# Second attentions of a two-layer kernel: one head of each pair scaled on VectorE, two bias tables and the latent norms in other places

## The chip, the cores and the metric

The kernel runs on one core of a Trainium2 chip. The metric is the device time of one execution in microseconds (us). All of the work is in float32.

## The reference, cut to what matters

The program computes two transformer blocks, one after the other, over 512 tokens of width 1024. The change lies in the mixing stage of the second block:

```python
z = rms_norm_2(h, mix_pre_g) @ w_in
q_na, k_na, v_na, c_q, c_kv, k_rope = jnp.split(z, split_at, axis=-1)
o_na = neighbourhood_attention(q_na, k_na, v_na, na_rpb)     # 8 heads
o_mla = latent_attention(c_q, c_kv, k_rope, ...)             # 8 heads
mixed = concat([rms_norm_2(o_na, g1), rms_norm_2(o_mla, g2)]) @ w_out

def latent_attention(...):
    q = rms_norm_2(c_q, q_norm_g) @ w_uq       # 256 -> 8 x 96
    kv = rms_norm_2(c_kv, kv_norm_g) @ w_ukv   # 128 -> 8 x 128
    q_rot, k_rot = apply_rope(q_rot), apply_rope(k_rope)
    p = softmax((qn @ k_nope.T + qr @ k_rot.T) * scale)
    return p @ v
```

In the neighbourhood attention a query sees 256 keys and each head adds a bias table made from `na_rpb`. In the latent attention a query sees all 512 keys.

## The kernel before, in words

Everything is written out by hand, one program for each engine, and the engines meet through counting semaphores. The tokens are four tiles of 128. Before the attentions the projections (`z2_psum`, `z2_evac`) run on TensorE in four groups n, each with two weight units of raw float32 that ScalarE (L402) and VectorE (L408) split into a high and a low part; three products (L417 to L419) make one float32 product. Units are numbered from `AT_MID`: 0 to 7 are `w_in`, 8 and 9 the latent up-projections, 10 to 13 `w_out`. SyncE loads a unit (`feed`, L714) once the unit two before it is split.

Both attentions ("na", the neighbourhood attention, then "mla", the latent attention) go through the same four functions, `attend_pe`, `attend_dve`, `attend_act` and `attend_pool`. A phase has 32 steps, one for a head and a tile of 128 queries. Round d (16 of them, and two more to drain, `LAG` is 2) takes steps 2d and 2d + 1, the same tile of the two heads of a pair. I call them head a and head b. In a round each engine does, in this order:

- TensorE: the transposes of the probabilities of round d - 2 (L542, waits for `scaled`), the score products of round d (L553, waits until both scores of round d - 1 are taken), and, once in four rounds, the head outputs from the transposed probabilities (L571).
- VectorE: score plus bias with the running maximum (L603) for step 2d; then the reciprocal (L583) of the sum of step 2d - 1; then L603 for 2d + 1; then the reciprocal of 2d. In rounds 5, 9, 13 and 17 it also takes the low part of a pair's output (L1848, L1851), and waits for TensorE and ScalarE before.
- ScalarE: copies of the transposes of round d - 2 (L635), then the exponentials of steps 2d and 2d + 1 with their sums (L645), and the high part of the output (L1484, L1486) in rounds 5, 9, 13 and 17.
- GpSimd: each step's probabilities times the reciprocal, in place (L660).

In the neighbourhood attention a bias table of a head is one product (L1306) and three additions on VectorE (L2115). Tables 0 and 1 come ahead of the rounds and table 2 at the opening of round 0, so three are made before the first score is taken. The others come two in four rounds. TensorE waits ahead of them for `band_in`: 32 transfers, issued by GpSimd (L957), that lay the values v2 out in bands (`Vband`). They must land before the attention because the probabilities buffer `PB2` lies where v2 was. VectorE in the meantime does the norms of the two latents: eight squares with sums (L2096), a square root on ScalarE, eight scalings (L2104).

Between the attentions come the transposes of the latents, the up-projections, the rotations of k and q on VectorE (L2133 to L2138; q's four tiles after the last copy of k, L2145) and the transposes per head (L1352). Then VectorE splits units 10 and 11 of `w_out` ahead of the first latent score.

## Time and profile before

| | us |
|---|---|
| median of three runs (lowest) | 2055.45 (2053.97) |
| profiled execution | 2055.96, of which span 2054.1 |
| first to last projection of the stage | about 1305 to 1391 |
| end of projections to the first neighbourhood score | 1391 to 1410 |
| neighbourhood attention, first score to last head outputs | 1410.1 to 1465.5 |
| norm sums, latent transposes and projections, rotations | 1469 to 1512 |
| latent attention, first score to last head outputs | 1518.0 to 1592.6 |

Times within the span count from its start. The stage with the change is about an eighth of the span. TensorE is busy 88% of the whole span but much less between 1391 and 1600.

### The profile page before, as it was taken

How to read it: one execution, taken by the hardware profiler on the slowest of the kernel's cores; microseconds unless marked ns; L12 is line 12 of the kernel's file. 1: busy time of each engine (PE TensorE's matmuls, PEld its weight loads, DVE VectorE, ACT ScalarE, POOL GpSimd, SP SyncE). 2: the span in 40 equal slices, each digit the busy share in tenths (PEclk: the TensorE clock that was granted, in tenths of full speed). 3: DMA queues.
4: the chain of work that ended last, by engine and by line, in shares of the span. 5: the costliest groups of instructions: out<-in, count | busy, mean ns of one | idle time of the engine just before them, and what ended most of it. 6: DMA issues, size and time to landing. Idle time of an engine off the chain costs nothing.

```text
span 2054.1 us, 22543 instructions
## 1 busy us (share of the span) xinstructions
PE 1816.5 (88%) x8515; PEld 1439.0 (70%) x8515; DVE 925.0 (45%) x1469; ACT 853.1 (42%) x1348; POOL 294.6 (14%) x374
## 2 busy tenths in 40 slices
PE   5996999999769999939999999696767959999996
PEld 4884666668658888828888887583643748888885
DVE  3446334334359999942322323525243352322324
ACT  3224565552348888832223222324456132223221
POOL 2100442220001111200000000623236000000000
PEclk9998899999779999969999999897789979999998
DMA  5223101115369999642324332331010113324321
GB/s 178 97 75 107 48 22 57 47 42 217 131 220 375 387 382 379 225 164 82 102 73 112 92 102 73 103 110 52 1 41 1 52 52 103 102 81 114 85 100 52
DMA packets 160930, 248.37 MB, mean 121 GB/s; under 512 B 11490, under 2 KB 117057, under 8 KB 147904
## 3 DMA queue, kind: packets, MB, share of 16 engines
q1 hardware_dynamic: 151056, 230.21, 33.2%
q0 software_dynamic: 9776, 16.86, 2.7%
q8 instruction: 62, 1.02, 0.2%
q14 instruction: 36, 0.29, 0.0%
HBM read 241.22 MB, written 12.61 MB: 124 GB/s over the span
## 4 chain that ended last, share of the span: by engine, by line
PE 84%; DVE 8%; issue 2%; ACT 2%; POOL 2%; DMA 2%; SPq 0%; DVEq 0%; ACTq 0%
PE psum L417 24%; PE psum L419 23%; PE psum L418 23%; PE psum L553 3%; PE psum L571 3%; PE psum L542 2%; POOL arena L660 2%; DVE tarea_r L1711 1%; DMA warea<-in_w_in 1%; DVE harea L1683 1%; ACT warea_r L402 1%; PE psum L1161 1%; DVE harea L1698 1%; DVE xarea L1700 1%; PE psum L1071 1%
## 5 line engine op out<-in xcount | busy, mean ns | idle before, releaser
L408 DVE TENSOR_TENSOR warea_r<-warea,warea_r 128x2048 fp32r<-128x2048 f32 x114 | 266.5, 2339 | 409.0 <-ACT warea_r L402 408.9
L417 PE MATMUL psum<-tarea_r,warea_r 128*128 128x512 f32 x896 | 358.3, 400 | 13.4 <-DVE tarea_r L1711 13.4
L418 PE MATMUL psum<-tarea_r,warea_r 128*128 128x512 f32 x896 | 352.6, 394 | 0.0
L419 PE MATMUL psum<-tarea_r,warea_r 128*128 128x512 f32 x896 | 352.2, 393 | 0.0
L402 ACT ACTIVATE warea_r<-warea 128x2048 fp32r<-128x2048 f32 x114 | 217.5, 1910 | 287.0 <-PE psum L419 282.6
L417 PE MATMUL psum<-warea_r,arena_r 128*128 128x512 f32 (+1 forms) x768 | 300.7, 392 | 12.1 <-DVE arena_r L2010 7.3
L419 PE MATMUL psum<-warea_r,arena_r 128*128 128x512 f32 (+1 forms) x768 | 297.1, 387 | 0.0
L418 PE MATMUL psum<-warea_r,arena_r 128*128 128x512 f32 (+1 forms) x768 | 297.0, 387 | 0.0
L417 PEld LDWEIGHTS psum<-tarea_r,warea_r 128*128 128x128 f32 x896 | 170.5, 190 | 54.5 <-DVE tarea_r L1711 14.1
L419 PEld LDWEIGHTS psum<-tarea_r,warea_r 128*128 128x128 f32 x896 | 170.5, 190 | 36.4
L418 PEld LDWEIGHTS psum<-tarea_r,warea_r 128*128 128x128 f32 x896 | 170.7, 190 | 33.9
L1573 ACT ACTIVATE arena<-psum 128x512 f32<-128x512 f32 x44 | 26.3, 599 | 370.2 <-PE psum L419 370.2
L417 PEld LDWEIGHTS psum<-warea_r,arena_r 128*128 128x128 f32 (+1 forms) x768 | 143.6, 187 | 44.0 <-DVE arena_r L2010 7.9
L419 PEld LDWEIGHTS psum<-warea_r,arena_r 128*128 128x128 f32 (+1 forms) x768 | 143.3, 187 | 29.3
L418 PEld LDWEIGHTS psum<-warea_r,arena_r 128*128 128x128 f32 (+1 forms) x768 | 143.6, 187 | 28.1
L2057 DVE TENSOR_TENSOR arena<-psum,arena 128x512 f32<-128x512 f32 x44 | 30.4, 692 | 290.4 <-ACT arena L1573 290.4
L417 PE MATMUL psum<-warea_r,tarea_r 128*128 128x512 f32 (+3 forms) x408 | 156.7, 384 | 1.4 <-DVE tarea_r L2126 1.4
L418 PE MATMUL psum<-warea_r,tarea_r 128*128 128x512 f32 (+3 forms) x408 | 155.8, 382 | 0.0
L419 PE MATMUL psum<-warea_r,tarea_r 128*128 128x512 f32 (+3 forms) x408 | 155.7, 382 | 0.0
L973 PE MATMUL psum<-const,harea 128*128 128x128 f32 x160 | 29.2, 368 | 86.6 <-DVE harea L1683 86.6
L660 POOL TENSOR_SCALAR arena<-arena,rr 128x256 f32<-128x256 f32 (+1 forms) x64 | 78.8, 1242 | 122.5 <-DVE rr L583 122.3
L635 ACT ACTIVATE harea<-psum 128x128 f32<-128x128 f32 (+4 forms) x192 | 73.6, 419 | 48.7 <-PE psum L542 48.0
(291 smaller groups left out, 2438.5 us busy)
## 6 DMA issues: line engine op xcount, KB each, us to landing
warea<-in_ffn_w_gu SPq DMA_DIRECT2D x88, 512.0 KB, 5.0
warea<-in_w_in SPq DMA_DIRECT2D x48, 512.0 KB, 4.6
warea<-in_ffn_w_down SPq DMA_DIRECT2D x40, 512.0 KB, 4.2
arena<-in_w_up SPq DMA_DIRECT2D x16, 1024.0 KB, 7.6
tarea<-in_w_up SPq DMA_DIRECT2D x16, 1024.0 KB, 7.1
tarea<-in_w_down SPq DMA_DIRECT2D x16, 1024.0 KB, 7.6
warea<-in_w_gate SPq DMA_DIRECT2D x14, 1024.0 KB, 7.5
harea<-in_w_gate SPq DMA_DIRECT2D x14, 1024.0 KB, 7.8
```

Of the source, the lines that this page charges most:

```text
L402: act.activation(w_hi[:, u % 2, :], raw[:, u % RAW, :], ACT.Copy).then_inc(s["split_hi"], 1)
L408: dve.tensor_tensor(w_lo[:, u % 2, :], raw[:, u % RAW, :], w_hi[:, u % 2, :].bitcast(f32), ALU.subtract)\
L417: nc.tensor.matmul(out, high, by_high, start=first, stop=False)
L418: nc.tensor.matmul(out, high, by_low, start=False, stop=False)
L419: return nc.tensor.matmul(out, low, by_high, start=False, stop=last)
L542: mm = nc.tensor.transpose(bank[0:rows, P * j:P * j + P], pbuf[:, c0:c0 + rows], ident)
L553: mm = nc.tensor.matmul(ps[st["e"]][:, a:b], st["lhsT"], rhs, start=True, stop=not (mask and b == n))
L571: mm = nc.tensor.matmul(half(bank, e_)[:, c:d_], lhsT, PT[0:lhsT.shape[0], e_, j, a:b], start=start, stop=stop)
L635: nc.scalar.activation(PT[0:rows, st["e"], 0:nj, st["dst"]:st["dst"] + P], src, ACT.Copy)\
L660: ins = nc.gpsimd.tensor_scalar(p, p, rr[:, k:k + 1], None, ALU.mult)
L973: mm = nc.tensor.transpose(ps[2 * t + half_][:, P * c:P * c + P], hn[:, t, P * (4 * half_ + c):P * (4 * half_ + c) + P], ident)
L2057: V.tensor_tensor(sgb[:, v % 2, :], ps[2 * (v % 2) + 1], sgb[:, v % 2, :], ALU.mult).then_inc(s["gated"], 1)
```

## The change

1. In the two second attentions head b's probabilities are scaled on VectorE, at the opening of the next round, ahead of that round's scores. GpSimd scales head a only. A new semaphore `scaled_dve` counts VectorE's, and `scaled(n)` tells who waits for which. The first attention keeps its order.
2. The neighbourhood tables 0 and 1 are multiplied in the last group of projections (into banks 0 and 1), and VectorE makes them before it splits units 8 and 9.
3. The latent norms go from ahead of the attention into its rounds: squares in rounds 2 to 5, the root in ScalarE's round 6, scalings in rounds 8 to 11.
4. The 32 band transfers go to SyncE's queue, behind unit 9; TensorE waits for them only ahead of the first head outputs. `PB2` and the scratch `zsq` move to the gain area, and `load_gain(5)` goes behind the attention.
5. q is rotated tile by tile during the up-projections; TensorE waits only for the last copy of k.
6. Units 10 and 11 are split inside the latent attention: ScalarE in rounds 2 and 5, VectorE in rounds 3 and 6.

```diff
-    v2, PB2 = carve(8192, NT, 512), carve(8192, 4, T)
+    v2, PB2 = carve(8192, NT, 512), whole(G_AT + 1024, 4, 256)
+    def scaled(n):
+        if n < alone:
+            return s["scaled"], n + 1
+        return (s["scaled_dve"], (n - alone) // 2 + 1) if (n - alone) % 2 else (s["scaled"], alone + (n - alone) // 2 + 1)
...
@@ attend_pe
-                    pe.wait_ge(s["scaled"], n0 + m + 1)
+                    pe.wait_ge(*scaled(n0 + m))
...
+                if ph["name"] == "na" and u == 0:
+                    pe.wait_ge(s["band_in"], 16 * 32)
...
@@ attend_dve
+            if n0 >= alone and 0 <= 2 * d - 1 < len(steps):
+                m = 2 * d - 1
+                recip(m)
+                p = ph["pb"][:, (n0 + m) % 4, 0:steps[m]["keys"]]
+                dve.wait_ge(s["recd"], n0 + m + 1)
+                nc.vector.tensor_scalar(p, p, rr[:, k:k + 1], None, ALU.mult).then_inc(s["scaled_dve"], 1)
             for m in range(2 * d, 2 * d + 2):
...
-                if 0 <= m - 1 < len(steps):
+                if 0 <= m - 1 < len(steps) and (n0 < alone or m % 2):
                     recip(m - 1)
...
@@ attend_pool
+            if n0 >= alone and m % 2:
+                continue
...
@@ sync
             for u in range(AT_MID, AT_FFN2):
                 feed(u)
+                if u == AT_MID + 9:
+                    sp.wait_ge(s["z2_evac"], 12)
+                    for b, band in enumerate((0, 8, 24, 32)):
+                        for r in range(8):
+                            sp.dma_start(Vband[...], v2[...]).then_inc(s["band_in"], 16)
...
@@ tensor
+                    if n == 3 and h == 0:
+                        pe.wait_ge(s["xrev_in"], 16 * 8 * H)
+                        for g in range(2):
+                            pe.wait_ge(s["z2_evac"], 8 + g + 1)
+                            na_table(g, ps[g])
-            pe.wait_ge(s["band_in"], 16 * 32)
+            pe.wait_ge(s["na_tab"], 2)
             attend_pe(pe, na, na_table)
...
-            pe.wait_ge(s["cn_ready"], 1)
+            pe.wait_ge(s["cn_ready"], 4)
...
-            pe.wait_ge(s["roped"], 2)
+            pe.wait_ge(s["roped"], 1)
...
@@ scalar
-            root(rstd[:, 16:24])
-            attend_act(act, na, pair_high(...))
+            def latent_root(d):
+                if d == 6:
+                    root(rstd[:, 16:24])
+            attend_act(act, na, pair_high(...), split=latent_root)
...
-            split_high(AT_MID + 10)
-            split_high(AT_MID + 11)
-            attend_act(act, mla, pair_high(...))
+            def out_high(d):
+                if d in (2, 5):
+                    split_high(AT_MID + 10 + d // 5)
+            attend_act(act, mla, pair_high(...), split=out_high)
...
@@ vector
-            for k in range(2, 10):
+            for k in range(2, 8):
                 split_low(AT_MID + k)
+            for g in range(2):
+                na_table(g, ps[g])
+            split_low(AT_MID + 8)
+            split_low(AT_MID + 9)
+            attend_dve(dve, na, pair_low(...), na_table, latent_norm)
...
             for t in range(NT):
+                dve.wait_ge(s["mla_evac"], 4 * t + 2)
+                rope(q_[:, :, 64:80], q_[:, :, 80:96], ct, st_, [P, H, 16], 128)
                 dve.wait_ge(s["mla_evac"], 4 * t + 4)
                 ins = V.tensor_copy(kf[...], view(z3[:, t, 384:416], [[0, H], [1, 32]]))
...
-            split_low(AT_MID + 10)
-            split_low(AT_MID + 11)
-            attend_dve(dve, mla, pair_low(...))
+            def out_low(d):
+                if d in (3, 6):
+                    split_low(AT_MID + 10 + d // 6)
+            attend_dve(dve, mla, pair_low(...), fill=out_low)
```

`latent_norm(d)` does for tile d - 2 the two squares (d 2 to 5), the variances (d 5), the inverse root (d 7) and for tile d - 8 the two scalings (d 8 to 11).

How this moves the instructions, on VectorE at the first scores of the neighbourhood attention. Before (L2104 is the last of the latent norms, L2115 a table, L603 a score, printed as ISA, with its maximum; L583 a reciprocal):

```order
L2104 SCALAR_TENSOR_TENSOR arena<-arena,rstd,small 128x128
L2106 MEMSET nmax 128x1
L2115 TENSOR_TENSOR arena<-psum,const 128x256 x9
L603 ISA arena,nmax<-psum,arena 128x256
L603 ISA nmax 128x1
L603 ISA arena,nmax<-psum,arena 128x256
L603 ISA nmax 128x1
L583 RECIPROCAL rr<-sums 128x1
L2115 TENSOR_TENSOR garea<-psum,const 128x256 x3
L603 ISA arena,nmax<-psum,arena 128x256
L603 ISA nmax 128x1
L583 RECIPROCAL rr<-sums 128x1
```

and of the changed kernel, from the split of the last projection units on (L408 the split, L2152 a table, L621 the score, L594 the reciprocal, L609 the new scaling, L2129 a latent's square):

```order
L408 TENSOR_TENSOR warea_r<-warea,warea_r 128x2048 x6
L2152 TENSOR_TENSOR arena<-psum,const 128x256 x6
L408 TENSOR_TENSOR warea_r<-warea,warea_r 128x2048 x2
L2152 TENSOR_TENSOR arena<-psum,const 128x256 x3
L621 ISA garea,nmax<-psum,arena 128x256
L621 ISA nmax 128x1
L621 ISA garea,nmax<-psum,arena 128x256
L621 ISA nmax 128x1
L594 RECIPROCAL rr<-sums 128x1
L2152 TENSOR_TENSOR garea<-psum,const 128x256 x3
L594 RECIPROCAL rr<-sums 128x1
L609 TENSOR_SCALAR garea<-garea,rr 128x256
```

Six table additions now stand ahead of the last two splits, three remain ahead of the first score, and head b's scaling stands ahead of the next score. Its round 2 from the scaling of round 1's head b to head b's reciprocal, with the first squares:

```order
L609 TENSOR_SCALAR garea<-garea,rr 128x256
L621 ISA garea,nmax<-psum,arena 128x256
L621 ISA nmax 128x1
L621 ISA garea,nmax<-psum,arena 128x256
L621 ISA nmax 128x1
L594 RECIPROCAL rr<-sums 128x1
L2129 ISA garea,ss<-arena 128x256
L2129 ISA ss 128x1
L2129 ISA garea,ss<-arena 128x128
L2129 ISA ss 128x1
L594 RECIPROCAL rr<-sums 128x1
```

The squares stand between the reciprocals of head a and head b.

VectorE in the latent attention, rounds 0 and 1. Before (L2156 copies of the transposes per head):

```order
L2156 COPY arena<-psum 96x512 x8
L408 TENSOR_TENSOR warea_r<-warea,warea_r 128x2048 x2
L603 ISA arena,nmax<-psum,arena 128x512
L603 ISA nmax 128x1
L603 ISA arena,nmax<-psum,arena 128x512
L603 ISA nmax 128x1
L583 RECIPROCAL rr<-sums 128x1
L603 ISA arena,nmax<-psum,arena 128x512
L603 ISA nmax 128x1
L583 RECIPROCAL rr<-sums 128x1
L603 ISA arena,nmax<-psum,arena 128x512
```

and now, from the scaling of round 2's head b to that of round 3, with the split of unit 10:

```order
L594 RECIPROCAL rr<-sums 128x1 x2
L609 TENSOR_SCALAR arena<-arena,rr 128x512
L621 ISA arena,nmax<-psum,arena 128x512
L621 ISA nmax 128x1
L621 ISA arena,nmax<-psum,arena 128x512
L621 ISA nmax 128x1
L594 RECIPROCAL rr<-sums 128x1
L408 TENSOR_TENSOR warea_r<-warea,warea_r 128x2048
L594 RECIPROCAL rr<-sums 128x1
L609 TENSOR_SCALAR arena<-arena,rr 128x512
```

The two splits no longer stand ahead of the first score; one stands between the reciprocals of head a and head b of round 3, the other likewise in round 6.

## Rows read from the trace of the kernel before

**Rows 1.** Three stretches by engine: us, busy time (x) of PE, PEld, DVE, ACT, POOL, PEclk, DMA share, GB/s
```profile
1390.00:1404.00 14.00, 2.47 (x7) 1.00 (x5) 9.85 (x32) 3.81 (x4) 0.00 (x0) 0.65 0.49 141
1425.00:1438.40 13.40, 10.19 (x71) 6.04 (x69) 7.38 (x34) 8.27 (x26) 7.29 (x8) 0.87 0.00 1
1538.70:1557.40 18.70, 14.75 (x67) 7.33 (x68) 7.22 (x26) 11.97 (x27) 12.41 (x8) 1.00 0.00 0
```

**Rows 2.** Timeline, VectorE and TensorE, from the projections to the first score (start us, us, what)
```profile
1393.24 2.29 DVE L408 TENSOR_TENSOR warea_r<-warea,warea_r 128x2048 fp32r<-128x2048 f32 x1 [7.06 <-ACT warea_r L402]
...
1399.53 3.60 DVE L2104 SCALAR_TENSOR_TENSOR arena<-arena,rstd,small 128x256 f32<-128x256 f32 x8
...
1404.30 1.65 PE L1306 MATMUL psum<-arena,const 128*128 128x384 f32 x2 [7.84 <-DVE arena L2115]
...
1405.99 1.09 DVE L2115 TENSOR_TENSOR arena<-psum,const 128x256 f32<-128x256 f32 x3 [1.74 <-PE psum L1306]
...
1410.06 0.42 DVE L603 CUSTOM_DVE_ANT_0 arena<-psum,arena 128x256 f32<-128x256 f32 x1 [0.16 <-DVE arena L2115]
```

**Rows 3.** Timeline of first rounds, neighbourhood attention: ScalarE, GpSimd, VectorE, TensorE
```profile
1411.04 0.49 ACT L645 ACTIVATE arena<-arena,nmax 128x256 f32<-128x256 f32 x1
...
1411.43 0.92 POOL L660 TENSOR_SCALAR arena<-arena,rr 128x256 f32<-128x256 f32 x1 [22.02 <-DVE rr L583]
...
1415.70 0.42 DVE L603 CUSTOM_DVE_ANT_0 arena<-psum,arena 128x256 f32<-128x256 f32 x1 [1.94 <-PE psum L553]
...
1416.30 1.82 POOL L660 TENSOR_SCALAR arena<-arena,rr 128x256 f32<-128x256 f32 x2 [1.38 <-DVE rr L583]
...
1417.37 0.66 PE L542 MATMUL psum<-const,arena 128*128 128x128 f32 x2 [1.08 <-POOL arena L660]
...
1417.96 1.22 PE L553 MATMUL psum<-arena 64*128 64x256 f32 x4
...
1419.21 0.42 DVE L603 CUSTOM_DVE_ANT_0 arena<-psum,arena 128x256 f32<-128x256 f32 x1 [2.25 <-PE psum L553]
```

**Rows 4.** Timeline, TensorE: last head outputs of the neighbourhood attention
```profile
1465.54 3.68 PE L571 MATMUL psum<-harea,arena 128*64 128x128 f32 x32 [0.47 <-ACT harea L635]
```

**Rows 5.** Timeline, VectorE and TensorE, between the latent projections and the latent attention
```profile
1495.40 0.29 DVE L2145 COPY harea<-arena 128x256 f32<-128x256 f32 x1 [3.18 <-ACT arena L1631]
...
1501.60 6.20 PE L1352 MATMUL psum<-const,arena 128*96 128x128 f32 x32 [6.92 <-DVE nmax L2152]
...
1512.36 1.96 PE L553 MATMUL psum<-arena 96*128 96x512 f32 x4 [0.83 <-ACT arena L1636]
...
1513.62 4.50 DVE L408 TENSOR_TENSOR warea_r<-warea,warea_r 128x2048 fp32r<-128x2048 f32 x2 [1.37 <-ACT warea_r L402]
...
1518.04 0.68 DVE L603 CUSTOM_DVE_ANT_0 arena<-psum,arena 128x512 f32<-128x512 f32 x1
```

**Rows 6.** Timeline, ScalarE, GpSimd, VectorE and TensorE in the latent attention
```profile
1519.40 3.78 PE L553 MATMUL psum<-arena 96*128 96x512 f32 x4 [5.08 <-DVE nmax L603]
...
1519.49 0.70 ACT L645 ACTIVATE arena<-arena,nmax 128x512 f32<-128x512 f32 x1
...
1519.87 1.57 POOL L660 TENSOR_SCALAR arena<-arena,rr 128x512 f32<-128x512 f32 x1 [55.14 <-DVE rr L583]
...
1533.83 0.69 DVE L603 CUSTOM_DVE_ANT_0 arena<-psum,arena 128x512 f32<-128x512 f32 x1 [2.36 <-PE psum L553]
...
1537.93 0.69 DVE L603 CUSTOM_DVE_ANT_0 arena<-psum,arena 128x512 f32<-128x512 f32 x1 [2.36 <-PE psum L553]
...
1592.62 5.07 PE L571 MATMUL psum<-harea,arena 128*64 128x512 f32 x16 [0.69 <-ACT harea L635]
```

**Rows 7.** Timeline, GpSimd and VectorE in the first projections
```profile
56.08 3.60 POOL L871 TENSOR_TENSOR harea<-arena 128x2048 f32<-128x2048 f32 x1 [41.58 <-ACT arena L1432]
...
57.83 4.00 DVE L408 TENSOR_TENSOR warea_r<-warea,warea_r 128x2048 fp32r<-128x2048 f32 x1 [8.94 <-ACT warea_r L402]
```

**Rows 8.** Timeline, SyncE: issues of transfers
```profile
1377.62 0.80 SPq L714 DMA_DIRECT2D warea<-in_mla_w_ukv  x2
```

More of the change, by code:

```diff
@@ L316, in build_blocks @@
     rpbs = carve(13312, 64)
-    zsq = whole(H_AT, 256)
+    zsq = whole(G_AT + 768, 256)
     z3 = carve(16144, NT, 416)
@@ L526, in attend_pe @@
         rounds = len(steps) // 2
-        if table:
+        if table and ph["name"] != "na":
             table(0)
@@ L580, in recip @@
             if n0 + n >= 8:
-                dve.wait_ge(s["scaled"], n0 + n - 7)
+                dve.wait_ge(*scaled(n0 + n - 8))
             k = (n0 + n) % 8
             nc.vector.reciprocal(rr[:, k:k + 1], sums[:, k:k + 1]).then_inc(s["recd"], 1)
-        if table:
+        if table and ph["name"] != "na":
             table(0)
@@ L616, in attend_act @@
         rounds = len(steps) // 2
-        if table:
+        if table and ph["name"] != "na":
             table(0)
@@ L1271, in _, with na_table @@
             pe.wait_ge(s["f_evac"], 16)
+            def na_table(g, bank=ps[7]):
+                if g >= H:
+                    return
+                if g >= 2:
+                    pe.wait_ge(s["na_tab"], g)
+                nc.tensor.matmul(bank[:, 0:384], flip, xrev[:, g, :], start=True, stop=True).then_inc(s["tab_psum"], 1)
             to_features(3)
@@ L1612, in _ @@
                 split_high(AT_MID + 2 * n + 3)
-            root(rstd[:, 16:24])
-            attend_act(act, na, pair_high(na, lambda pair: o2[0][0][:, pair, :], 984, sq_na))
+            def latent_root(d):
+                if d == 6:
+                    root(rstd[:, 16:24])
+            attend_act(act, na, pair_high(na, lambda pair: o2[0][0][:, pair, :], 984, sq_na), split=latent_root)
             root(rstd[:, 24:28])
@@ L2089, in _ @@
             low_features(3)
-            for k in range(2, 10):
+            for k in range(2, 8):
                 split_low(AT_MID + k)
-            dve.wait_ge(s["z2_evac"], 16)
-            for t in range(NT):
-                for k, (a, b_) in enumerate(((0, 256), (256, 384))):
-                    ins = V.tensor_tensor_reduce(out=zsq[:, 0:b_ - a], in0=z3[:, t, a:b_], in1=z3[:, t, a:b_], scale=1.0,
-                                                 scalar=0.0, op0=ALU.mult, op1=ALU.add, accum_out=ss[:, 16 + 4 * k + t:17 + 4 * k + t])
-                    chained(ins)
@@ L2099, in _ @@
-            chained(variance(rstd[:, 16:20], ss[:, 16:20], 256))
-            variance(rstd[:, 20:24], ss[:, 20:24], 128).then_inc(s["var_ready"], 1)
-            inverse_root(rstd[:, 16:24])
-            for t in range(NT):
-                for k, (a, b_) in enumerate(((0, 256), (256, 384))):
-                    chained(V.scalar_tensor_tensor(out=z3[:, t, a:b_], in0=z3[:, t, a:b_], scalar=rstd[:, 16 + 4 * k + t:17 + 4 * k + t],
-                                                   in1=small[:, 600 + a:600 + b_], op0=ALU.mult, op1=ALU.mult))
@@ L2109, in na_table @@
+            def na_table(g, bank=ps[7]):
                 if g >= H:
```

59 lines of the change are left out of this document (33 added, 26 removed).

## Prediction

> **What bounds the kernel now.** I read the page first, then the chain of waits between 1390 and 1650 us, the busy times by stretch, and last the timelines of single rounds. The chain runs through TensorE in the rest of the kernel, and the change does not touch that. Between 1391 and 1600 it does not: in the four rounds from 1538.7 to 1557.4 TensorE is busy 14.75 of 18.7 us, and GpSimd, VectorE and ScalarE less still [rows 1]. No engine is full, so a loop of waits sets the round.
>
> In the neighbourhood attention the loop is this: VectorE takes a score at 1415.70, does head b's reciprocal behind it, GpSimd starts at 1416.30 (head b of the round before, then head a; 1.82 for both), TensorE transposes at 1417.37, multiplies the next scores from 1417.96 for 1.22, and VectorE's next score comes at 1419.21 [rows 3]. That is 3.5 us; the four rounds from 1425 took 13.4, so 3.35 each with tables and a head output [rows 1]. The point to see is that head b's reciprocal stands behind a score of the next round, which stands behind TensorE. In the latent attention the same loop takes 4.10 (1533.83 to 1537.93) [rows 6].
>
> Ahead of the attentions VectorE alone is on the chain. Its last split ends at 1395.5, the latents' norms end at 1403.1, and three tables at 1.09 each, each with a product of 1.65 in front, put the first score at 1410.06 [rows 2]. Before the latent attention there are two more such places: after the last copy of k at 1495.40 the rotations of q keep TensorE until 1501.60, and two splits keep the first latent score from about 1513.4 until 1518.04 [rows 5].
>
> **The change, part by part.** Gains have a minus.
>
> *Opening, -11.6.* The norms (7.6) and two of three tables leave the stretch. Two products join the projections ahead of the last split. At 1.65 each [rows 2], a time taken at a lower clock, they cost 3.3, at twice the clock half of it; the projections keep TensorE full, so I take 1.8. VectorE's two tables there have idle time to lie in (7.06 ahead of the last split [rows 2]). The last split then ends at 1395.5 + 1.8 = 1397.3, table 2 at 1398.4, and the first score is 11.6 earlier than 1410.06.
>
> *The new operation.* No row shows a scaling on VectorE from SBUF to SBUF. Nearest below is the copy of 128x256 in 0.29 [rows 5], above the scores at 0.42 and 0.69 [rows 2, 6]. I take 0.35 for 256 columns and 0.49 for 512, near the copy, with a little for the scalar's operand.
>
> *Does it wait for GpSimd?* In the first projections a split that takes 2.29 elsewhere [rows 2] took 4.00: it started at 57.83 while GpSimd worked from 56.08 to 59.68, and ended at 61.83, about 2.2 after GpSimd [rows 7]. So VectorE stood still until GpSimd was done. This split reads two SBUF inputs; the scaling reads one. But the copy gets 256 columns through in 0.29 where the score takes 0.42, so it uses a wider path than the score, and I take it that the wide path is the one shared. The Trainium skill says the same (SBUF — State Buffer, Who interferes with whom): GpSimd's only ports are VectorE's second pair, two-input operations and the fast form of one-input ones need it, and the first to start holds it for the whole instruction. By that rule the trace's 4.00 agrees, and the change puts the two halves of a pair on engines that can't work at once. Without the rule's one-input half the sum would be rival 1's.
>
> *A plain neighbourhood round, 2.64.* From a score to GpSimd's start 1.37 (1410.06 to 1411.43), GpSimd 0.92 [rows 2, 3], then head b's scaling 0.35, then the next score. Head b's exponential (from 1411.04) is done at about 1.60 after the score and its reciprocal at 1.76, so without the wait for GpSimd it would be 2.15. TensorE fits below: transposes 0.66 and scores 1.22 [rows 3], both released by the round before.
>
> *All neighbourhood rounds, +4.8.* Fifteen rounds at 2.64 are 39.6. Six tables lie mostly beside GpSimd: 0.3 each, 1.8. Three rounds with a head output hold VectorE behind TensorE and ScalarE as before, and the scaling comes on top: 2.2 each, 6.6. The latents' squares and scalings read two SBUF inputs, so each pair stands around GpSimd's 0.92: I take 1.1 in each of eight rounds, 8.8 (their bare work, 7.6 from 1395.5 to 1403.1 [rows 2], less what lies in idle time, is the lower bound at about 3; a GpSimd operation's 0.92 ahead of both of a pair, 1.82, the upper, 14.6). From the last score to the last head outputs 3.5 (2.64 and a transpose and a copy). Sum 60.3, against 1410.06 to 1465.54, 55.5 [rows 2, 4]. So the rounds get longer although the loop gets shorter, since 16 operations were moved into them. The root adds table loads on ScalarE; its idle time covers them. The bands' 32 issues at 0.40 [rows 8] end near 1391, and the first head outputs come after 1410: nothing.
>
> *Rotations, -5.8, and -1.* TensorE's transposes start 0.4 after the copy at 1495.40 in place of 1501.60 [rows 5]. With 6.9 less of idle time ahead, its clock should be better for the first of them (6.20 for 32): -1, between 0 and -2.
>
> *Latent opening, -4.6.* The two splits, 4.50, go. The scores' products start at 1512.36, the first head's half is done at 1513.4 [rows 5], and the score follows.
>
> *Latent rounds, -0.6.* Plain: 1518.04 to 1519.87 is 1.83, GpSimd 1.57, scaling 0.49: 3.89 against 4.10 [rows 5, 6]. Fifteen are 58.4. Three head outputs 1.8 each, 5.4 (before, 18.7 less three times 4.10 gives 6.4 for such a round; now 5.7, as TensorE is ahead). The two splits now stand between the reciprocals of a round, and GpSimd and VectorE take turns around 2.29: 2.5 each, 5.0 (0 if all is covered, 4 if GpSimd's turn comes whole on top). Tail 5.2. Sum 74.0 against 74.6 (1518.04 to 1592.62) [rows 5, 6].
>
> Sum: -11.6 + 4.8 - 5.8 - 1 - 4.6 - 0.6 = -18.8. The profiled execution took 2055.96, so 2037; the median of the runs, 2055.45, is the same within 0.5.
>
> **Rivals.**
>
> 1. *The scaling does not wait for GpSimd, the two-input operations do.* For it: the only row shows a two-input operation. Against: the copy's speed. A plain latent round is then 1519.49 + 0.80 for head b's sum, 2.3 after the score, reciprocal, scaling: 3.0; TensorE, busy 14.75 in four rounds with a head output [rows 1], needs about 3 in a plain one and makes it 3.1. The 15 rounds save 0.8 each, less what the splits take back: 7 more. The neighbourhood saves 1.5, since its rounds hold the latents' operations. -27: 2029.
> 2. *No operation waits for GpSimd there.* Then the latents' and splits' prices shrink too, 6 more: 2023. Rows 7 speak against it.
> 3. *Slower: TensorE falls to the lower clock in the latent attention.* In the neighbourhood rounds 10.19 busy of 13.4 went with 0.87, in the latent ones 14.75 of 18.7 with 1.00 [rows 1]. At the lower clock the scores' products take 3.78 [rows 6], twice their usual time, transposes grow too, and TensorE needs about 5.4 for a round: at 1.5 over 3.89, 15 rounds cost 23 more, the head outputs 6. -18.8 + 29 = +10: 2066. It turns to a loss from two thirds of that attention at 1.2 GHz on. Against it: the new rounds hold the same products in less time, so TensorE rests less.
> 4. *The bands come late.* If SyncE took 1.5 for a transfer in place of 0.40, they would land at 1428, and the first head outputs, due near 1414, would wait 14: 2051. It decides from 1.1 each on.
>
> **How the numbers follow.** Forecast 0.60; rival 1 0.20; rival 2 0.07; rival 3 0.05; rival 4 0.08. The forecast's own range is 2030 to 2044 (latents 3 to 14.6, splits 0 to 4 more, the tables' product 0.9 to 3.3, clock). The range reaches to rival 2 below and rival 4 above: 2022 to 2051. Two per cent are 41 us, about what a measurement of this kernel can tell from no change. No case but a sum of several goes beyond: faster 0.02, slower 0.01, within 0.97.
>
> **What would show it.** First neighbourhood score at about 1398; plain rounds 2.6 there with the scaling starting when GpSimd ends (longer than 0.35, as its record would include the wait); rounds 2 to 5 and 8 to 11 longest; last head outputs at about 1459. Transposes per head start 0.4 after the last copy of k. Plain latent rounds 3.9, rounds 3 and 6 over 6. A latent round near 3.1 with GpSimd and the scaling side by side would be rival 1; a split or a square at its bare time beside GpSimd rival 2; TensorE at 1.2 GHz there rival 3; TensorE waiting for a transfer ahead of the first head outputs rival 4. I am wrong in the main term if the first score doesn't come before 1400.

## The result, and the profile after

The changed kernel takes 2022.4 us (median of 4 runs, 2020.4 to 2023.3) against 2055.1 for the kernel before on the same chip: a ratio of 0.984, 95% interval 0.982 to 0.986. One of the four runs of before took 3139.5 us, which the ratio leaves out; the median of the other three is 2054.7. The profiled execution of after, the longest of its four, has a span of 2021.5, 32.6 less than before's.

The two kernels do not enter the changed part at the same time, though nothing ahead of it differs. So the stages are counted from a common mark, VectorE's weight split at 1375.30 before and 1374.08 after, the third from last of the projections, to the first split behind both attentions (1616.78 and 1585.29). This *stretch* is 241.5 us before and 211.2 after, 30.3 less. The rest of the 32.6 lies ahead of it (1.2) and behind it (1.1).

| Stage | before | after | measured | predicted |
|---|---|---|---|---|
| mark to first score | 34.8 | 22.5 | -12.3 | -11.6 |
| neighbourhood rounds, to the last head outputs | 55.5 | 55.5 | 0.0 | +4.8 |
| to the transposes per head | 36.1 | 30.3 | -5.8 | -5.8 |
| to the first latent product | 10.8 | 8.4 | -2.4 | -1 |
| to the first latent score | 5.7 | 1.2 | -4.5 | -4.6 |
| latent rounds, to the last head outputs | 74.6 | 68.9 | -5.7 | -0.6 |
| to the first split behind | 24.2 | 24.4 | +0.2 | no term |

The timeline of after at these borders (start, duration, engine, line, operation, idle time before it and who ended it). It is to be held against [rows 2, 4, 5]:

```profile
1393.37 2.29 DVE L408 TENSOR_TENSOR warea_r<-warea,warea_r 128x2048 fp32r<-128x2048 f32 x1 [7.79 <-ACT warea_r L402]
1396.58 0.41 DVE L621 CUSTOM_DVE_ANT_0 garea<-psum,arena 128x256 f32<-128x256 f32 x1
...
1452.10 3.68 PE L582 MATMUL psum<-harea,arena 128*64 128x128 f32 x32 [0.47 <-ACT harea L653]
...
1482.06 0.29 DVE L2190 COPY harea<-arena 128x256 f32<-128x256 f32 x1 [0.20 <-ACT arena L1658]
1482.40 0.32 PE L1376 MATMUL psum<-const,arena 128*96 128x128 f32 x1 [1.14 <-DVE harea L2190]
...
1490.78 1.53 PE L562 MATMUL psum<-arena 96*128 96x512 f32 x3 [0.82 <-ACT arena L1663]
...
1492.01 0.69 DVE L621 CUSTOM_DVE_ANT_0 arena<-psum,arena 128x512 f32<-128x512 f32 x1 [1.33 <-PE psum L562]
...
1560.92 1.08 PE L582 MATMUL psum<-harea,arena 128*64 128x512 f32 x4 [0.74 <-ACT harea L653]
```

See that only 0.9 us lie between the last split's end at 1395.66 and the score, where before had norms and tables, that the transposes start 0.34 after the last copy does, and that the latent score no longer has two splits ahead of it.

A plain neighbourhood round, to be held against [rows 3]: GpSimd's scaling and VectorE's new one run side by side.

```profile
1400.95 0.16 DVE L594 RECIPROCAL rr<-sums 128x1 f32<-128x1 f32 x1 [0.32 <-ACT garea L663]
1401.21 1.03 POOL L680 TENSOR_SCALAR garea<-garea,rr 128x256 f32<-128x256 f32 x1 [2.35 <-DVE rr L594]
...
1401.64 0.35 DVE L609 TENSOR_SCALAR garea<-garea,rr 128x256 f32<-128x256 f32 x1
1401.94 0.42 DVE L621 CUSTOM_DVE_ANT_0 garea<-psum,arena 128x256 f32<-128x256 f32 x1
```

VectorE starts 0.43 us into GpSimd's operation and is through in 0.35; GpSimd takes 1.03 where it took 0.92 before. The prediction had VectorE starting only when GpSimd ends (1402.24). A latent round shows the same at 512 columns, and then the round with the first output split, to be held against [rows 6]:

```profile
1496.78 1.59 POOL L680 TENSOR_SCALAR arena<-arena,rr 128x512 f32<-128x512 f32 x1 [1.28 <-DVE rr L594]
...
1497.43 0.49 DVE L609 TENSOR_SCALAR arena<-arena,rr 128x512 f32<-128x512 f32 x1
1497.83 0.68 DVE L621 CUSTOM_DVE_ANT_0 arena<-psum,arena 128x512 f32<-128x512 f32 x1
...
1500.71 0.69 DVE L621 CUSTOM_DVE_ANT_0 arena<-psum,arena 128x512 f32<-128x512 f32 x1
...
1503.65 2.27 DVE L408 TENSOR_TENSOR warea_r<-warea,warea_r 128x2048 fp32r<-128x2048 f32 x1
1503.83 3.53 POOL L680 TENSOR_SCALAR arena<-arena,rr 128x512 f32<-128x512 f32 x1 [2.58 <-DVE rr L594]
...
1506.04 0.72 DVE L609 TENSOR_SCALAR arena<-arena,rr 128x512 f32<-128x512 f32 x1
1506.68 0.68 DVE L621 CUSTOM_DVE_ANT_0 arena<-psum,arena 128x512 f32<-128x512 f32 x1
```

Score to score is 2.88 (1497.83 to 1500.71) where before took 4.10. But the split, 0.18 ahead of GpSimd, holds it off: 3.53 instead of 1.59, and that round takes 5.97.

ScalarE in the round with the latents' root has two function loads on the chain:

```profile
1418.72 1.28 ACT L1418 ACT_TABLE_LOAD   x1
1420.01 0.21 ACT L1418 ACTIVATE rstd<-rstd 128x8 f32<-128x8 f32 x1
1420.13 0.64 ACT L653 ACTIVATE harea<-psum 128x256 f32<-128x256 f32 x2
1420.78 1.28 ACT L663 ACT_TABLE_LOAD   x1
1422.08 0.51 ACT L663 ACTIVATE garea<-garea,nmax 128x256 f32<-128x256 f32 x1
```

The exponential at 1422.08 is of the score at 1419.20; the next round's score comes 5.5 us after that one. Last, the busy times by stretch (sum, busy us of TensorE, its weight loads, VectorE, ScalarE, GpSimd, granted clock, DMA share, GB/s), beside [rows 1]:

```profile
1482.40:1490.80 8.40, 7.57 (x65) 6.55 (x65) 5.49 (x8) 5.38 (x9) 0.00 (x0) 1.00 0.00 0
1490.80:1531.20 40.40, 32.98 (x122) 16.75 (x122) 24.59 (x67) 27.06 (x57) 18.47 (x9) 0.92 0.16 53
1531.20:1562.00 30.80, 27.18 (x127) 13.53 (x128) 15.17 (x51) 20.86 (x48) 11.67 (x9) 1.00 0.05 17
```

### The profile page after: what moved, and what is told of

Same layout as the page of the kernel before. It is cut to its first block, busy times and chain, and to the rows that moved or that the text cites. A ratio compares the mean times of both kernels' runs of the same rounds, so it can differ in the third digit from the quotient of the medians.

```text
span 2021.5 us, 22548 instructions
## 1 busy us (share of the span) xinstructions
PE 1809.7 (90%) x8515; PEld 1434.7 (71%) x8515; DVE 936.8 (46%) x1499; ACT 851.2 (42%) x1350; POOL 246.7 (12%) x310
## 4 chain that ended last, share of the span: by engine, by line
PE 83%; DVE 7%; ACT 3%; issue 3%; DMA 2%; POOL 1%; SPq 0%; DVEq 0%; ACTq 0%; POOLq 0%
PE psum L417 24%; PE psum L418 23%; PE psum L419 23%; PE psum L562 3%; PE psum L582 3%; PE psum L551 2%; ACT warea_r L402 1%; DVE tarea_r L1741 1%; DMA warea<-in_w_in 1%; PE psum L1182 1%; DVE harea L1728 1%; DVE xarea L1730 1%; PE psum L1092 1%; DVE harea L1713 1%; POOL arena L680 1%
## 5 line engine op out<-in xcount | busy, mean ns | idle before, releaser
L408 DVE TENSOR_TENSOR warea_r<-warea,warea_r 128x2048 fp32r<-128x2048 f32 x114 | 266.5, 2338 | 402.7 <-ACT warea_r L402 402.6
L417 PEld LDWEIGHTS psum<-tarea_r,warea_r 128*128 128x128 f32 x896 | 170.0, 190 | 54.2 <-DVE tarea_r L1741 14.1
L562 PE MATMUL psum<-arena 64*128 64x256 f32 (+3 forms) x416 | 87.3, 447 | 2.7 <-DVE nmax L621 1.9
L417 PEld LDWEIGHTS psum<-warea_r,tarea_r 128*128 128x128 f32 x408 | 78.5, 192 | 15.2 <-DVE tarea_r L2167 1.8
```

The source lines that it names most:

```text
L408: dve.tensor_tensor(w_lo[:, u % 2, :], raw[:, u % RAW, :], w_hi[:, u % 2, :].bitcast(f32), ALU.subtract)\
L417: nc.tensor.matmul(out, high, by_high, start=first, stop=False)
L562: mm = nc.tensor.matmul(ps[st["e"]][:, a:b], st["lhsT"], rhs, start=True, stop=not (mask and b == n))
```

## The experiments

Each run has the kernel before beside it (2055.3 to 2055.5 us). The *stretch* is counted as above in each run's own trace; after has 211.2. It is that of one execution, and not always of a middle one: the profiled execution of after is the longest of its four, those of e6, e7 and e9 are the shortest of theirs. So the column and the medians can differ by some us.

| Run | us, median | stretch | against after |
|---|---|---|---|
| e1 GpSimd scales both heads | 2037.4 | 225.9 | +14.7 |
| e2 norms ahead | 2022.6 | 211.3 | +0.1 |
| e3 root without loads | 2022.4 (one) | 209.6 | -1.6 |
| e4 splits ahead | 2023.1 | 209.0 | -2.2 |
| e5 late splits | 2014.6 | 202.8 | -8.4 |
| e7 late splits, early root | 2014.4 | 200.6 | -10.6 |
| e8 split behind GpSimd | 2027.6 (one) | 214.6 | +3.4 |
| e9 rotations behind the copies | 2029.4 | 215.0 | +3.8 |
| e10 first tables behind the splits | 2024.6 (one) | 214.9 | +3.7 |
| e6 before, with VectorE's scaling | 2033.9 | 220.4 | -21.0 against before |

**Who holds whom, by itself.** For each pair of operations a short action of ScalarE releases both engines; three or six one-column reciprocals ahead put VectorE's later.

> Leaves out the whole computation (the output is a copy of some input rows) and only times VectorE and GpSimd operations alone and started together or one behind the other: on VectorE a scaling of 512 or 2048 columns in place, a two-input subtraction of 512 or 2048 columns, and one that reads PSUM; on GpSimd a 512-column scaling or a two-input product. Theory A (what the trace after shows): a scaling on VectorE takes 0.49 us for 512 columns whether or not GpSimd's scaling (1.57) runs beside it, and GpSimd's grows by 0.1 at most; a two-input operation of VectorE that has started holds GpSimd's scaling off for all its length (2.27 + 1.4 for 2048 columns), and one that starts later than GpSimd's is hardly held. Rival B (what the prediction took): whichever starts first holds the other for its whole instruction, so the 512-column scaling behind a GpSimd scaling takes 1.0 to 1.9 us. Rival C: it depends on GpSimd's operation: beside the one-input scaling VectorE is free, beside the two-input product each VectorE operation is held to its end.

Alone, the scaling of 512 columns took 0.49 on VectorE and 1.58 on GpSimd; of 2048 columns 1.29 on VectorE; the two-input subtraction of 512 and 2048 columns 0.69 and 2.29; GpSimd's two-input product 1.26. The timeline of the pairs (L26 and L28 scaling of 512 and 2048, L32 two inputs of 2048, L40 GpSimd's scaling, L42 its product):

```profile
39.10 0.49 DVE L26 TENSOR_SCALAR va<-va,vs 128x512 f32<-128x512 f32 x1 [2.45 <-ACT at L79]
39.16 1.87 POOL L40 TENSOR_SCALAR ga<-ga,gs 128x512 f32<-128x512 f32 x1 [0.45 <-ACT at L79]
...
41.48 1.56 POOL L40 TENSOR_SCALAR ga<-ga,gs 128x512 f32<-128x512 f32 x1 [0.45 <-ACT at L79]
42.01 0.49 DVE L26 TENSOR_SCALAR va<-va,vs 128x512 f32<-128x512 f32 x1
...
52.69 2.28 POOL L40 TENSOR_SCALAR ga<-ga,gs 128x512 f32<-128x512 f32 x1 [0.45 <-ACT at L79]
53.22 1.29 DVE L28 TENSOR_SCALAR va<-va,vs 128x2048 f32<-128x2048 f32 x1
...
73.23 2.29 DVE L32 TENSOR_TENSOR vc<-va,vb 128x2048 f32<-128x2048 f32 x1 [2.46 <-ACT at L79]
73.30 3.67 POOL L40 TENSOR_SCALAR ga<-ga,gs 128x512 f32<-128x512 f32 x1 [0.45 <-ACT at L79]
...
77.42 1.56 POOL L40 TENSOR_SCALAR ga<-ga,gs 128x512 f32<-128x512 f32 x1 [0.45 <-ACT at L79]
...
77.95 2.30 DVE L32 TENSOR_TENSOR vc<-va,vb 128x2048 f32<-128x2048 f32 x1
...
98.53 1.26 POOL L42 TENSOR_TENSOR gc<-ga,gb 128x512 f32<-128x512 f32 x1 [0.74 <-ACT at L79]
99.08 0.99 DVE L26 TENSOR_SCALAR va<-va,vs 128x512 f32<-128x512 f32 x1
...
132.23 1.26 POOL L42 TENSOR_TENSOR gc<-ga,gb 128x512 f32<-128x512 f32 x1 [0.43 <-ACT at L79]
132.78 2.85 DVE L32 TENSOR_TENSOR vc<-va,vb 128x2048 f32<-128x2048 f32 x1
```

GpSimd's one-input scaling, once it runs, holds neither of VectorE's (42.01, 77.95). When VectorE is first it holds GpSimd to its own end, 1.44 us of GpSimd's work staying behind it (39.16: 0.43 + 1.44; 73.30: 2.22 + 1.45). GpSimd's two-input product does hold VectorE, one input or two, until it is done: +0.50 and +0.56. So A stands for the operations of this kernel, C for GpSimd's product, and B falls: the prediction's scaling would have taken 1.5. One pair does not go by who is first: VectorE's scaling of 512 columns, its record 0.04 ahead of GpSimd's product, took 1.58 and ended 0.28 behind it, while the two-input subtractions with the same lead took 0.69 and 2.29 and held the product. A subtraction that read one input from PSUM held nobody and was held by nobody (0.69 in each of its eight pairs).

**The scaling back on GpSimd.** One line: `alone` covers all steps, so that VectorE scales none.

```
-    alone = len(phases[0]["steps"])
+    alone = n_steps
```

> The kernel after with both heads' scalings of a round on GpSimd again; everything else stays. Theory A (the split over two engines is the core of the gain, since GpSimd's two scalings of 0.92 or 1.57 us end last in a round): plain rounds of the latent attention go from 2.88 back to 4.1, their sum from 68.9 to 75 to 80 us, those of the neighbourhood attention from 55.5 to 60 to 66; 2022.4 becomes 2034 to 2044. Rival B (the prediction's: the scaling waits for GpSimd, and VectorE's part is worth 0.2 us a latent round and nothing in the neighbourhood's): plain latent rounds at 2.9 to 3.1, 2020 to 2026.

+15.0 us in the medians, +14.7 in the stretch. From the first to the last score the latent rounds take 72.6 instead of 63.5, the neighbourhood rounds 55.2 instead of 51.4. Plain latent rounds are back at 4.10. In the timeline GpSimd's two scalings are one block of 3.10, the transposes wait for its first half and the next score for TensorE:

```profile
1497.81 3.10 POOL L680 TENSOR_SCALAR arena<-arena,rr 128x512 f32<-128x512 f32 x2
...
1499.52 0.63 PE L551 MATMUL psum<-const,arena 128*128 128x128 f32 x4 [1.07 <-POOL arena L680]
...
1501.05 0.69 DVE L621 CUSTOM_DVE_ANT_0 arena<-psum,arena 128x512 f32<-128x512 f32 x1 [2.36 <-PE psum L562]
```

A is right, B falls.

**That part alone, on the kernel before.** The same lines as in the change's first part, nothing else.

> The kernel before with the first part of the change alone: a round opens with VectorE's scaling of the last step, GpSimd keeps one head of a pair. Theory A (the one part that makes the rounds shorter; its undoing cost 15 us): latent rounds plain 2.9 us instead of 4.1 and their sum 62 to 63.5 instead of 74.6, neighbourhood rounds 49 to 52 instead of 55.5: 2036 to 2042. Rival B (the prediction's terms: the scaling waits for GpSimd): latent rounds 3.9 plain, neighbourhood rounds no shorter, 2053 to 2055.

2033.9 us, ratio 0.990 (0.988 to 0.991), 21 us under before. First to last score: latent rounds 56.7 instead of 67.6, neighbourhood rounds 41.4 instead of 50.9, a little better than A's. So this part alone brings two thirds of what the whole change does, and taking it out of the whole change costs 15 (e1); the prediction had 0.2 us a latent round for it.

**The norms ahead.** Edit: the twelve pieces of `latent_norm` run in a row ahead of `attend_dve`, the root ahead of `attend_act`.

> The kernel after with the latents' norms (squares, root, scalings) ahead of the first table of the neighbourhood attention's rounds instead of inside them. Theory A: the norms ahead put the first score off by about 8 us (squares 3.5, scalings 3.3, the root between), and the rounds, rid of the root's two function loads (3 us) and of the squares and scalings where VectorE has no idle time (3 to 5 us), fall from 55.5 to 48 to 50: 2022.4 becomes 2023 to 2026. Rival B (VectorE's idle time covers the norms, and ScalarE's the loads): rounds stay at 53 to 55.5, 2028 to 2031. Rival C (the norms cost as much inside as ahead, 8.8 us, as the prediction had it): 2021.5 to 2023.

The first score comes 6.7 us later (9.9 behind the last split's start instead of 3.2), the rounds from first to last score take 44.9 instead of 51.4, 6.6 less. In all nothing: rival C, the prediction's view that the norms cost as much inside as ahead, is right, at 6.6 instead of 8.8 (A had the shorter rounds right, 49.0 to the last head outputs, and the later first score too high). VectorE is busy 36.4 of the 55.5 us of after's rounds, but its idle time is time in which the loop waits for ScalarE and TensorE, and what is put ahead of a score there pushes the loop. Of the 6.6, 2.9 lie in the one distance between scores that has the root's loads (5.50 against 2.63). The squares of rounds 2 and 3 cost nothing: these rounds take 2.72 and 3.68 with them and without.

What they wait for is seen beside e6, which also has no norms in the rounds. Its rounds 2 and 3 take 2.06 and 2.63, at a granted clock of 1.00; those of e2 had 0.50, and four score products take 1.22 us instead of 0.70. The 15 distances from score to score add up to 44.9 in e2 and 41.4 in e6, so the lower clock has 3.4 us of the neighbourhood rounds, and after's rounds 0 to 3 ran at 0.50 to 0.53 as well.

**The root's loads.** The square root is left out, a copy in its place:

```
-                    root(rstd[:, 16:24])
+                    nc.scalar.activation(rstd[:, 16:24], rstd[:, 16:24], ACT.Copy).then_inc(s["root_ready"], 1)
```

> The kernel after with the latents' root left out of the computation: ScalarE copies the eight columns at the same place (round 6 of the neighbourhood attention) instead of taking their square root, so that no function is loaded there and none behind it. Theory A (the two loads of 1.28 us stand on the chain of that round, since ScalarE's next two exponentials wait behind them): the distance of the scores of rounds 7 and 8, 5.5 us (1419.20 to 1424.70), falls to 2.6, all else as after, the span from 2021.5 to about 2018.6. Rival B (VectorE's table and TensorE's products of that round fill the same time): it falls by less than 1.

The distance falls from 5.5 to 3.46 (1418.95 to 1422.41): -2.0, not the 2.9 of A, as TensorE's scores are then the last to come. The stretch gained 1.6, the one time nothing: behind the latent rounds, from the last score to the next split, it needed 32.7 us where after needed 29.7, with a granted clock of 0.50 in five of them where after had 1.00 (e8, below, shows the same).

**The output splits ahead of the latent rounds**, as before the change:

```
-                if d in (3, 6):
-                    split_low(AT_MID + 10 + d // 6)
...
+            split_low(AT_MID + 10)
+            split_low(AT_MID + 11)
```

> The kernel after with the two weight units of the output split ahead of the latent attention's rounds on ScalarE and VectorE, as before, instead of in rounds 2, 3, 5 and 6. Theory A (the split holds GpSimd's scaling, 1.57 to 3.53 us, for over 2 us, and the round behind it runs its products at a lower TensorE clock): rounds 3 and 6 fall from 5.97 and 5.3 to about 2.9 and 4.0, those behind them from 4.3 to 3.0, the sum from 68.9 to 61 to 63; the first score comes 4 to 5 us later; 2022.4 becomes 2019 to 2021. Rival B (the prediction's 2.5 us a split, nothing behind): sum 64, 2022 to 2023.

The two splits, 4.49 in one block from 1492.87, put the first latent score off by 4.5 (14.1 behind the transposes' start instead of 9.6), and the rounds, first to last score, take 56.9 instead of 63.5. So in this pair of runs a split in the rounds cost 3.3, against 2.25 ahead. But e4's rounds are not free of a cost of the splits either: the first two distances are 3.47 and 4.41, at a granted clock of 0.52 and 0.60, where after has 2.94 and 2.88 at 1.00. Against e5, below, whose rounds run at 1.00 throughout (54.7), the splits cost after's rounds 8.8, and e4 4.5 ahead and 2.2 in the rounds. In time nothing is shown: A had 2019 to 2021, the median is 2023.1 against 2022.4, and of the 2.2 in the stretch the two profiled executions have 0.5 left at the end.

**The hold in the kernel.** Four chained one-column reciprocals (0.74 us) stand ahead of `split_low` in rounds 3 and 6.

> The kernel after with four one-column reciprocals of VectorE, each waited for (0.19 us each, as measured by themselves), ahead of its two splits in the latent rounds, so that GpSimd's scaling, released 0.2 us before the split in after, has run for 0.5 us when the split starts. Theory A (the hold hangs on who is there first: started 0.5 us ahead, GpSimd's scaling took 1.56 and the 2048-column two-input operation 2.30, neither longer than alone): GpSimd's scaling in rounds 3 and 6 takes 1.6 us instead of 3.53, the split 2.3; the transposes that waited 2.2 us for GpSimd start at once. The price of the split in its round hardly falls, since VectorE's next scores stand behind the split itself: rounds 3 and 6 within 0.8 us of 5.97 and 5.32. Rival B (a running GpSimd operation is held in a kernel where other engines work too, or the hold is what the round pays): scaling over 3 us again, or rounds 3 and 6 shorter by 1.5 us and more.

```profile
1504.72 1.57 POOL L680 TENSOR_SCALAR arena<-arena,rr 128x512 f32<-128x512 f32 x1 [2.58 <-DVE rr L594]
...
1505.32 2.29 DVE L408 TENSOR_TENSOR warea_r<-warea,warea_r 128x2048 fp32r<-128x2048 f32 x1
1506.43 0.63 PE L551 MATMUL psum<-const,arena 128*128 128x128 f32 x4 [0.28 <-POOL arena L680]
```

With GpSimd 0.6 ahead nobody is held: 1.57 and 2.29. Rounds 3 and 6 take 6.5 and 5.9 (0.6 more, the delay), those behind them 2.9 and 3.2 instead of 4.2 and 4.4. It looks as if the hold were paid a round later, but e3 and e9 say otherwise. There GpSimd is held as in after and TensorE waits 2.24 us for it, and yet the round behind round 3 takes 2.88, as in e8. TensorE's transposes in that round in after:

```profile
1507.50 1.94 PE L551 MATMUL psum<-const,arena 128*128 128x128 f32 x8 [2.23 <-POOL arena L680]
```

and e9's hold and transposes:

```profile
1509.33 3.53 POOL L680 TENSOR_SCALAR arena<-arena,rr 128x512 f32<-128x512 f32 x1 [2.58 <-DVE rr L594]
...
1513.00 1.06 PE L551 MATMUL psum<-const,arena 128*128 128x128 f32 x8 [2.24 <-POOL arena L680]
```

The granted clock of that round was 0.60 in after and 1.00 in e3, e8 and e9; behind round 6, too, the rounds at 1.00 (e2) take 2.87 and those at 0.61 (after) 4.37, with the same hold. So what the round behind a split pays is the clock, and the hold by itself costs the next round nothing; the split costs its own length in its round. Why the clock fell in after and not in e9, where TensorE had been busy for the same 3.46 of 5.97 us, stays open.

The latent rounds won 1.0 in all. And yet the stretch is 3.4 longer, since TensorE's granted clock was 0.50 in the five microseconds of the last head outputs and 0.76 behind them; after had 1.00 and 0.83 (window of e8, then of after):

```profile
1561.00:1566.00 5.00, 4.51 (x12) 1.44 (x14) 0.00 (x0) 0.43 (x1) 0.00 (x0) 0.50 0.18 64
```

```profile
1561.00:1566.00 5.00, 4.30 (x23) 1.71 (x23) 0.17 (x1) 1.36 (x3) 0.00 (x0) 1.00 0.18 64
```

**The rotations of q behind the copies again.** The second wait of TensorE and the old loop come back.

> The kernel after with the rotations of q behind the last copy of k's rotated part again, all four ahead of the transposes per head. Theory A (the prediction's term: four rotations of 1.4 to 1.5 us stand wholly between the last copy and the first transpose when they are behind it): last head outputs to transposes per head 30.3 to 36.1 us, the transposes at a lower TensorE clock again (6.2 us for 32 instead of 3.8), together 6 to 8 us: 2028.5 to 2030.5. Rival B (TensorE's clock and the transposes take part of it back): under 5, below 2027.

2029.4, ratio 0.988 (0.986 to 0.989), 7.0 over after: A. The first latent score is 6.9 later after the mark (124.8 against 117.9); the transposes' first 32 take a median of 0.42 each instead of 0.27, at a granted clock of 0.58 instead of 1.00, behind 6.9 us in which TensorE idled for VectorE. The profiled stretch has only 3.8 of it: this execution, the shortest of its four, had latent rounds 1.5 shorter and an end 1.6 shorter than after's.

**The first two tables behind the splits again.** TensorE's two products leave the projections and go through one bank.

> The kernel after with the first two tables of the neighbourhood attention made behind the projections and behind VectorE's last splits, through one bank, as before; norms stay in the rounds. Theory A: the second table's product waits for the first table (product 0.9 at full clock, 1.65 at the lower, two tables of 1.25 to 1.3), while the projections are rid of two products (1.5 to 1.8 us): first score 3 to 5 us later after the last split than the 3.2 of after, net 1.5 to 3.5: span 2023 to 2025. Rival B (the products in the projections cost nothing and the opening is on the tables alone): net 4 to 6.

The last split comes 1.35 earlier after the mark (17.9 instead of 19.3), the price of two products; the first score lies 9.2 behind it instead of 3.2. Net +4.6 to the first score, +3.7 in the stretch, +2.1 in time (one run against a median). No theory is right as it stands: the products do cost 1.35, as A says and B denies, but the first score is 6.0 later behind the split where A had 3 to 5; the time lies in A's range and the first score in B's. In this run the third product starts at 1392.95 only, after 4.2 us of waiting for VectorE's table.

**A better place for the splits.** ScalarE's in rounds 5 and 9, VectorE's in rounds 9 and 13, all ahead of the pair's evacuation, where both engines wait for head outputs.

```
+            if fill and n0 > alone:
+                fill(d)
             u = unit_ends(ph, d)
             if u is not None and ph["units"][u]["last_of_pair"]:
                 evac(u)
...
-                if d in (3, 6):
-                    split_low(AT_MID + 10 + d // 6)
+                if d in (9, 13):
+                    split_low(AT_MID + 10 + d // 13)
```

> The kernel after with the two splits of output weights put where a pair's head outputs keep TensorE busy: ScalarE's in rounds 5 and 9 and VectorE's in rounds 9 and 13, each ahead of the pair's evacuation (VectorE idles 3.9 us there, ScalarE 2.05). The splits in rounds 2, 3, 5 and 6 of after cost 6.6 us against none in the rounds (last experiment: 63.5 against 56.9 from the first to the last score). Theory A (a hold of GpSimd and of VectorE costs only where a round waits for them; beside the head outputs it is hidden): first to last score 57 to 58.5 us with the first score as after, 2015.5 to 2017.5. Rival B (GpSimd's scaling, 3.5 instead of 1.57 us, is late for the transposes two rounds on, or the split's end is late for the next scores): 1.5 to 2.5 us a split stay, 2019 to 2021.

2014.6 us, ratio 0.9801 (0.9785 to 0.9818), 7.8 under after and below the range of A. The round with a split:

```profile
1520.74 3.65 PE L582 MATMUL psum<-harea,arena 128*64 128x512 f32 x16
...
1521.87 2.27 DVE L408 TENSOR_TENSOR warea_r<-warea,warea_r 128x2048 fp32r<-128x2048 f32 x1
1522.05 3.52 POOL L684 TENSOR_SCALAR arena<-arena,rr 128x512 f32<-128x512 f32 x1 [1.28 <-DVE rr L594]
...
1524.33 1.09 PE L551 MATMUL psum<-const,arena 128*128 128x128 f32 x8
```

GpSimd is held as before, 3.52, but TensorE has 3.65 us of head outputs meanwhile and its transposes come without a gap. First to last score 54.7, less even than with the splits ahead; in the window of the rounds TensorE is busy 52.56 of 55.40 us at a clock of 1.00, against 55.75 of 64.20 at 0.95 in after. Every plain round takes 2.88 (the first 2.94) and every round with head outputs 6.69, with a split or without one, so here the splits cost nothing:

```profile
1490.40:1545.80 55.40, 52.56 (x222) 25.27 (x221) 37.85 (x113) 43.51 (x96) 27.80 (x15) 1.00 0.12 39
```

**And the root earlier.** On top of it the squares in rounds 1 to 4, the root in round 5 between ScalarE's copies and exponentials, and a spare exponential behind it.

> The late splits of the run above, and the squares one round earlier (rounds 1 to 4), with the root in round 5 between ScalarE's copies and exponentials, where it idles 1.9 us (1410.4 to 1412.38) for VectorE's scores, and a one-column exponential of a spare column right behind the root, which brings the exponential's function back in the same gap. Theory A: of the 2.9 us that the root's loads cost in round 6, about 0.9 stays (2.8 us of loads and root in a gap of 1.9): 2 us under the run above, 2013.5 to 2015.5. Rival B (the squares, a round earlier, push the tables and scores by as much, or ScalarE's delay in round 5 meets the pair's evacuation): no better than the run above, within 0.5.

The neighbourhood rounds, first to last score, take 49.9 instead of e5's 51.9, the 2 us of A, and the stretch is 2.3 shorter. The medians say 2014.4 against 2014.6, with the runs spread over 5.6 and 2.5 us: unclear. Both beat after and before.

## Why the prediction was right or wrong

The time fell inside the range (2022 to 2051), at its lower edge, and the change is within 2%, as given. But the forecast of 2037.0 was 14.6 too slow, the result lies outside the 2030 to 2044 that the forecast gave itself, and its mechanism was wrong. That the stated range holds it is luck: its lower end was there for rival 2.

*Right, with their sizes:* the opening (-11.6 for -12.3), the rotations (-5.8 for -5.8; e9 says 7 with the clock), the latent opening (-4.6 for -4.5), the new operation's bare time (0.35 and 0.49, both to the digit), the norms' price being the same in the rounds as ahead (e2), the bands from SyncE (0.67 an issue, not 0.40, but over at 1398.6, and the first head outputs at 1410.50 did not wait). For the clock behind the rotations it had -1 and got -2.4, past its bound of -2: the first 32 transposes took 0.27 us each at a clock of 1.00, 3.8 in all instead of 6.20 [rows 5].

*The step that failed* is "Does it wait for GpSimd?". Rows 7 were read rightly, VectorE stood until GpSimd was done; but the operation there is GpSimd's two-input product, and the one that the change puts beside VectorE is GpSimd's one-input scaling. The single measurement had two properties, and the prediction carried the hold over by the wrong one: it asked what kind of operation VectorE has, and not what kind GpSimd has. The pairs show both. The Trainium skill (SBUF — State Buffer, Who interferes with whom) says that whoever issues first gets the shared pair of ports for the whole instruction. Here the trace disagrees on GpSimd's scaling: VectorE's takes 0.35 and 0.49 beside it, where the rule makes it wait 0.6 and 0.9 more.

From this step came the two mis-sized terms. *A plain neighbourhood round*, 2.64, is 2.08 (1399.86 to 1401.94): 15 of them, -8.4. *All neighbourhood rounds* were +4.8, which this would make -3.6, and came to 0. The norms are not the reason, they cost 6.6 with the root's loads and not 8.8 (e2). Tables cost 0.6 each and not 0.3 (2.63 against 2.05 in e6), though there are five of them in the rounds and not six: 1.1 more. The tail took 4.1 and not 3.5. The largest part, some 4, had no term: rounds at a granted clock of 0.50, of which e2 against e6 shows 3.4. The root's loads, which were to lie in ScalarE's idle time, cost 2.0 of the norms' 6.6 (e3): a load lies in idle time only if what stands behind it on its engine is not what the round waits for.

*Latent rounds*, -0.6: plain 3.89 was 2.88, -15.1 for 15. Of this 5.1 were left, because a round with head outputs now costs 3.8 more than a plain one (6.69 against 2.88) where 1.8 was taken, 6.0 for three, and the splits 8.8 together (against e5) where 5.0 was. Of the 8.8, 5.5 lie in the splits' own rounds (5.97 and 5.32 for 2.88), near the 5.0, and 3.3 in the rounds behind them, at a granted clock of 0.60 and 0.61, for which there was no term. With the loop of waits gone TensorE is what a round waits for: in e5 it is busy 52.56 of 55.40 us.

*The rivals.* Rival 1 (VectorE's scaling is free, 2029) had the plain latent round near 3.1, which is 2.88, and what it says of the scaling is what the runs show. Its time was too long because it took 1.5 off the forecast's neighbourhood rounds, where 4.8 came off; and the two-input operations are not held by GpSimd's scaling, they hold it when they are first. Rival 2 (2023) is nearest in time and in what VectorE does. It was given 0.07, on one row. Rivals 3 and 4 did not come: the latent rounds had the clock at 0.92 and 1.00 on the whole (single rounds at 0.60), and the first head outputs did not wait for the bands.

## What to carry to other kernels

Before a hold between two engines is taken from a trace into a forecast, the row must match in both operations, number of inputs and who comes first; if it doesn't, it is a bound and not the value. In a loop of waits an idle engine's time is not free: norms put into the rounds cost what they cost ahead (6.6 us), splits at least as much (8.8 against 6.7, the clock included), and nothing in e5; such work belongs where another engine, here TensorE with its head outputs, is sure to be busy for longer. A gain of 1 to 2 us can be gone at the end through the granted clock, so it must be read stage by stage.

## What the hardware showed that was not expected

- GpSimd's one-input scaling (1.56 us for 512 columns) is sensitive at its ends. A 512-column scaling of VectorE started 0.53 behind it delays nobody; one started 1.12 behind it, which covers its end, takes 0.72 instead of 0.49 (in e7 one of 256 columns that covers the end takes 0.58 instead of 0.35); one of 2048 columns that covers its end makes GpSimd's last 0.46 us wait (2.28). The two-input subtraction in the same places delays nobody. Why the end matters to one and not to the other, no run shows.
- Order decides: VectorE's two-input operation 0.07 ahead of GpSimd's scaling adds 2.1 us to it, 0.5 behind it nothing. A delay of 0.74 us bought off a hold of 2.0 (e8), and nothing was won by it: the round itself takes 0.6 more, and the next one, at a granted clock of 1.00, 2.88 with the hold (e3, e9) and without.
- TensorE's granted clock differs between kernels that do the same work at the same place, and it moved more than several of the edits: 0.60 or 1.00 in the round behind the first split after the same 3.46 us of work in 5.97 (4.24 or 2.88 us), 0.50 or 1.00 in neighbourhood rounds 2 and 3 (e2 and e6, 1.7 us together), and 0.50 or 1.00 in the same five microseconds at the end (e3 and e8 against after), there after rounds in which TensorE was busy for 3.4 of 5.6 us at 0.84 to 0.89 rather than 2.8 at 1.00. The last was worth up to 4.5 us of the stretch. What made it fall stays open.
